# The residual's x read from HBM into the residual's own tile, nine of sixteen tiles during the gate stage

## What is computed

```python
h = rmsnorm(x, g_mix)
proj = h @ w_in                                   # 2048 -> u (1024) | v (1024) | z (1024)
u, v = gelu(u), gelu(v)
out_a = u * (tril(W_s) @ rmsnorm_per_head(v) + b) # chunks of 128 positions, 8 heads
out_b = (pool(z) @ w_pool) * pool_scale           # trailing means over 2/4/8/16, minus the token
x = x + concat(out_a, out_b) @ w_out              # the residual that the change touches
h = rmsnorm(x, g_ffn)
x = x + square(relu(h @ w_up)) @ w_down           # 2048 -> 8192 -> 2048
return rmsnorm(x, g_final)
```

## Time and profile before

| | us |
|---|---|
| time, median of 3 runs | 1242.95 (1240.61 to 1244.18) |
| the profiled execution's own time | 1238.04 |
| its span, slowest core (0) | 1236.2 |
| spans of the eight cores | 1229.5 to 1236.2 |
| TensorE busy | 1193.5 (97% of the span) |
| VectorE / ScalarE / GpSimd busy | 354.9 / 221.0 / 78.8 |
| output projection of core 0, about | 212 to 330 |

### The profile page before, as it was taken

One profiled execution on the slowest core, in us unless ns is written; L12 is line 12 of the kernel. 1 busy time (PEld: TensorE's weight loads), 2 busy tenths in 40 slices (PEclk: granted clock), 3 DMA queues, 4 the chain that ended last, 5 costly groups with the idle time before them and its releaser, 6 DMA issues.

```text
span 1236.2 us, 14873 instructions; the slowest of 8 cores (1229.5 to 1236.2 us)
## 1 busy us (share of the span) xinstructions
PE 1193.5 (97%) x5880; PEld 571.5 (46%) x5984; DVE 354.9 (29%) x587; ACT 221.0 (18%) x446; POOL 78.8 (6%) x107
## 2 busy tenths in 40 slices
PE   4899999989999999999999999999999999999996
PEld 2354444434444444444444444444444444444585
DVE  3466646333322121111112121212121212121254
ACT  2401155133321100001111000111100011111233
POOL 0100022100000000000000000000000000010000
PEclk9999999999999999999999999999999999999998
DMA  9995640987533443344334443444334433446033
GB/s 271 232 183 76 83 83 2 145 168 173 127 69 68 83 88 68 68 77 93 70 69 73 91 76 68 70 86 83 69 68 85 85 69 69 81 81 111 26 125 124
DMA packets 36755, 118.59 MB, mean 96 GB/s; under 512 B 2768, under 2 KB 5200, under 8 KB 35664
## 3 DMA queue, kind: packets, MB, share of 16 engines
q0 software_dynamic: 22736, 87.04, 41.0%
q1 hardware_dynamic: 13376, 29.43, 7.5%
q10 hardware_dynamic: 576, 1.18, 0.3%
HBM read 196.28 MB, written 8.39 MB: 166 GB/s over the span
## 4 chain that ended last, share of the span: by engine, by line
PE 92%; DMA 5%; DVE 1%; issue 1%; SPq 1%; ACT 0%; DVEq 0%; ACTq 0%
PE ps L226 83%; PE ps L672 6%; DMA xstage<-xT 3%; DMA xf<-xT 2%; PE ps L412 1%; PE ps L896 1%; SPq L244 0%; PE ps L324 0%; PE ps L546 0%; DVE ostage L925 0%; PE ps L363 0%; SPq L248 0%; DVE xr_h L679 0%; PE ps L709 0%; DVE xr_h L883 0%
## 5 line engine op out<-in xcount | busy, mean ns | idle before, releaser
L226 PE MATMUL ps<-h2T,ringall 128*128 128x512 bf16 x2008 | 440.7, 379 | 2.1
L226 PEld LDWEIGHTS ps<-h2T,ringall 128*128 128x128 bf16 x2048 | 200.4, 98 | 241.6
L226 PE MATMUL ps<-pooled,ringall 128*128 128x512 bf16 (+1 forms) x989 | 212.1, 362 | 1.0
L226 PE MATMUL ps<-uT,ringall 128*128 128x512 bf16 (+1 forms) x992 | 212.1, 362 | 0.8
L804 DVE SCALAR_TENSOR_TENSOR rtmp<-ps,rstd_bc 128x512 f32<-128x512 f32 x128 | 82.4, 686 | 361.3 <-PE ps L226 350.0
L226 PEld LDWEIGHTS ps<-pooled,ringall 128*128 128x128 bf16 x1008 | 98.6, 98 | 101.9
L226 PEld LDWEIGHTS ps<-uT,ringall 128*128 128x128 bf16 x1008 | 98.5, 98 | 101.9
L809 ACT ACTIVATE uT<-rtmp 128x512 bf16<-128x512 f32 x64 | 39.1, 629 | 504.6 <-DVE rtmp L804 504.5
L226 PE MATMUL ps<-hT,ringall 128*128 128x512 bf16 x375 | 82.6, 379 | 0.6 <-issue 0.2
L809 ACT ACTIVATE pooled<-rtmp 128x512 bf16<-128x512 f32 x64 | 39.2, 629 | 181.8 <-DVE rtmp L804 181.8
L226 PEld LDWEIGHTS ps<-hT,ringall 128*128 128x128 bf16 x384 | 37.2, 98 | 44.4
(11 more groups left out here) (117 smaller groups left out, 624.6 us busy)
## 6 DMA issues: line engine op xcount, KB each, us to landing
ringall<-w_up POOLq DMA_DIRECT2D x32, 1024.0 KB, 8.0
ringall<-w_down POOLq DMA_DIRECT2D x29, 1024.0 KB, 7.9
ringall<-w_in POOLq DMA_DIRECT2D x10, 1024.0 KB, 12.6
xf<-xT SPq DMA_DIRECT2D x8, 1024.0 KB, 20.6
xstage<-xT SPq DMA_DIRECT2D x16, 512.0 KB, 10.0
ringall<-w_out POOLq DMA_DIRECT2D x7, 1024.0 KB, 17.2
wstg<-w_in SPq DMA_DIRECT2D x4, 1024.0 KB, 16.4
wres<-w_down POOLq DMA_DIRECT2D x3, 1024.0 KB, 22.1
```

The costliest lines, as they stand in the source:

```text
L226: ins = e.matmul(ps[:, banks[sel], c0:c1], lhsT, rhs, start=st, stop=sp_)
```

## The change

Two things. The destination: x of tile m is read into `XR(m)` itself for m = 3 to 15, and the evacuation adds the PSUM bank to it in place. Tiles 0, 1 and 2 keep a staging buffer, the two old ones and a third, `xs2`, which lies over `sqr` (the buffer of squares, not in use between the first norm's sums and the second's). The time of issue: nine loads (tiles 0, 1, 2, 4, 5, 6, 7, 8, 9) are issued one behind the other at `pool_all`, early in the gate stage; tile 3's when the last v projection has read `hT` (`h_dead`); and tiles 10 to 15 together when tile 3 has been evacuated and its matmuls have read `wx`. Each load has a semaphore of its own. The number of loads and their bytes stay as they are.

```diff
+    xs2 = sb("xs2", [128, TOK], F32, cur[0] - 4096)
...
-    xs_reader = [pool_all, pool_all]
+    def XS(m):
+        return (xstage[0][:, :], xstage[1][:, :], xs2[:, :])[m] if m < 3 else XR(m)
+
     xs_ld = {}
 
-    def load_xs(m):
-        xs_ld[m] = P.dma("sp", lambda e: e.dma_start(out=xstage[m % 2][:, :].rearrange("p (h t) -> p h t", h=2), in_=xT_d[:, :, m, :]),
-                         "xs%d" % (m % 2), [xs_reader[m % 2]])
-
-    for m in range(2):
-        load_xs(m)
+    def load_xs(m, deps):
+        xs_ld[m] = P.dma("sp", lambda e: e.dma_start(out=XS(m).rearrange("p (h t) -> p h t", h=2), in_=xT_d[:, :, m, :]), "xs%d" % m, deps)
+
+    for m in (0, 1, 2, 4, 5, 6, 7, 8, 9):
+        load_xs(m, [pool_all, sq_reader[2], sq_reader[3]])
+    load_xs(3, [h_dead])
...
-        ev = P.add("dve", lambda e: e.tensor_tensor(out=XR(m)[:, c0:c1], in0=ps[:, bank, :], in1=xstage[m % 2][:, c0:c1], op=ALU.add),
+        ev = P.add("dve", lambda e: e.tensor_tensor(out=XR(m)[:, c0:c1], in0=ps[:, bank, :], in1=XS(m)[:, c0:c1], op=ALU.add),
                    [job, xs_ld[m], h_dead, pool_all])
...
         if half == 1:
-            xs_reader[m % 2] = x1_e[1][m]
-            if m + 2 < KC:
-                load_xs(m + 2)
+            if m == HEAD:
+                for i in (10, 11, 12, 13, 14, 15):
+                    load_xs(i, [x1_e[1][m], h_dead, job])
             wo_norm(m)
```

## The result

| | before | after |
|---|---|---|
| time, median of 6 runs, us | 1242.55 | 1232.6 |
| range of the comparable runs, us | 1239.9 to 1244.2 | 1232.2 to 1234.3 |
| ratio (95% interval) | | 0.9926 (0.991 to 0.9942) |
| the profiled execution's own time, us | 1238.04 | 1232.2 |
| spans of its eight cores, us | 1229.5 to 1236.2 | 1227.8 to 1230.3 |

The medians are over all six runs, with one slow run on either side (1324.8 and 1371.9 us) that the range and the ratio leave out. By the ratio the change makes the kernel 0.74% faster (0.58 to 0.9%), about 9.2 us.

The account below looks back on a forecast made before the run. The prediction took staging's loop of evacuation and late x loads to stop TensorE in the output projection. Stops and clock gave -5.5 us, the rest 0: 1242.95 to 1237.4 us, range 1234.0 to 1241.7.

Parts of the forecast that it names:

- What bounds the kernel: Output projection: evacuation, load through full queues and later evacuation form a loop that stops TensorE; core 0's excess 5.52 us.
- the floor: Matmuls behind the last mixing to first up matmul: 97.62 us on core 5, without waits for evacuation.
- the remainder: First up matmul to the span's end: about 906 us, the same to within 0.5 us whenever it starts.
- In place costs nothing: Evacuation adding into the residual's tile keeps its pace; 0 to 1 ns on each of 32 instructions.
- the nine loads are covered: Gate stage: 3.67 MB more, all in by about 191, covered by idle DMA from 170 to 212; cost nothing.
- the six come in time: Tiles 10 to 15, issued about 242.2: last lands about 270, at worst 309, each at least 14 us early.
- the slabs are not starved: Output projection: weight slabs 15, 16 and 17 land before tiles 8 and later need them, without stops too.
- The sum: -5.5 us for stops and clock, 0 for the rest; 4.9 us between profiled execution and median taken as unaffected.
- Rival (b): More than the whole: the 4.9 us are longer stops of the same kind; gain 7 to 10 us, chance 0.14.
- (a): Less than the whole: the typical slowest core is slow for another reason; gain 0 to 3.7 us, chance 0.17.
- (c): Slower: the six x loads starve the weights, TensorE stops at tile 8; +4 us, 1247, chance 0.05.
- (d): Some x, say tile 3's, is still late and the stop moves; about no change, 1242 us, chance 0.03.

Follow-up runs that it names:

- lower-group: Executions of the unchanged kernel before between 1234.7 and 1238.7 us: 33 of the study's 68 comparable ones.
- upper-group: Executions of the unchanged kernel before between 1239.4 and 1245.7 us: 35 of the study's 68 comparable ones.
- e10: The kernel before, unchanged, profiled a third more time to catch a slow execution; 1242.58 us.
- e7: The changed kernel with x of tile 14 issued late on purpose, when tile 14's matmuls are done; 1237.63 us.
- e3: The changed kernel with the loads of tiles 3 to 9 issued together at h_dead instead of in the gate stage; 1232.42 us, ratio 0.9945.
- e4: The kernel before with a third staging buffer, loads three tiles ahead, nothing in place; ratio 0.9945, six of seven runs 1232.4 to 1232.7 us.
- e2: The changed kernel's in-place reads, but each load issued at its time in the kernel before; median 1241.95 us, ratio 1.0007.
- e9: The kernel before, unchanged, profiled a second more time; 1236.12 us.

## Why the prediction was right in its mechanism and wrong in its size

The loop of staging, load and evacuation and its stops for banks were read rightly. A second stop that comes of the same lag, the one for the squares, was missed, and with it the size.

**What bounds the kernel, the floor, the remainder**: right. The stretch is 97.56 us after (97.62 forecast as floor), the rest 906.35, and the profiled execution's forecast of 1232.5 is the median after.

**In place costs nothing; the nine loads are covered; the six come in time; the slabs are not starved**: right. On core 2 tiles 10 to 15 landed by 245.7 + 25.9 = 271.6 (270 taken), 17 us and more before their needs, and slab 17 at 230.6 + 26.3 = 256.9, earlier than the 262.1 of the earlier trace rows. Tile 3's load, issued at 211.1, took 4.0 us. Only the issue of the nine was off: not done at 154 but at 166.6, as single issues took up to 7.4 us instead of 0.54. Nothing stood behind them but tile 3's load, which was not due before 211.

**The sum**: this step failed. "I take them as unaffected", of the 4.9 us between the profiled execution and the median, had no row behind it, and they were nearly all of the same cause: 5.5 us was the loss of the worst core in a lower-group execution, and the runs that the median came from were upper-group. Rival (b) came near, time 1233 to 1236 with 0.14, but with the wrong mechanism: it priced one more stop for a bank, 3.9 us. What the runs show is a stop for the squares, 5.0 us of idle time in e10, 2.5 to 3.9 us in e7, with about 1.5 us of clock behind it. Core 6 of e10 lost 1240.7 - (226.71 + 97.56 + 906.35) = 10.1 us: stops of 1.99, 0.38 and 4.96, 0.45 for modelled ends, 0.65 and 1.07 for the slower matmuls behind the last stop (1.68 and 8.14 us against 1.03 and 7.07), and 0.6 that I can't assign.

That the miss came out as large as it did is in part the luck of the sample. All five comparable runs of the kernel before in the result are of the upper group, while of all 68 about half are; against the mixed sets of e3 and e4 the same time of 1232.4 to 1232.5 us is a gain of 0.55%, some 7 us. So the forecast's gain of 5.5 us was that of a lower-group execution, the measured 9.2 us is that of upper-group ones, and a typical mixture lies between.

**The row that was there to be read.** I followed TensorE's stops and stopped at the last one, 272. On core 0 that was the end of it. Core 6 of the same trace, on which the prediction used only TensorE's rows, had VectorE still waiting for x at the end:

```profile
313.26 1.29 DVE L679 TENSOR_TENSOR xr_h<-ps,xstage 128x512 f32<-128x512 f32 x2 [7.54 <-DMA xstage<-xT]
...
322.01 1.29 DVE L679 TENSOR_TENSOR xr_h<-ps,xstage 128x512 f32<-128x512 f32 x2 [3.79 <-DMA xstage<-xT]
...
325.33 1.22 DVE L718 TENSOR_TENSOR sqr<-sqacc,sqr 128x1024 bf16<-128x1024 f32 x1
```

```profile
327.87 1.03 PE L709 MATMUL ps<-sqr,ones 128*128 128x512 bf16 x4
```

322.01 is tile 14. The squares were ready at 325.33 + 1.22 = 326.55, and TensorE took up their sum at 327.87. This core was 1.3 us from the edge. A wait that ended just in time on one core of this execution was, in e10, the stop that set the time.

**The other rivals.** (a), less than the whole, (c), starved slabs, and (d) did not come. Against (a) the prediction said that the order of the spans is the order of the loss; that holds for the three cores that it shows and not for all eight (core 3 lost 1.8 us in the stretch and core 1 only 1.0, yet core 1's span is the longer, as its stretch began later). For (c), e3, which put seven x loads right ahead of the slabs, is the harder test, and it didn't come there either.

What stays open: why an execution is in the lower or the upper group. The lag begins with x loads of 15 to 22 us beside the four slabs, and their times differ by a few us from core to core; what decides them was not tried. Upper-group executions were traced twice only (e10, and e2 core 4 of the kernel in place at the old times). Nor was it tried to add up tile 13's squares on VectorE ahead of tile 14's evacuation, which would test the stop for the squares with the staging buffers left alone.

## What to carry to other kernels

A double buffer whose refill waits for its reader can keep the lag that one crowded stretch gives it, when refill and evacuation beside other traffic take about as long as the work that they cover (14.0 and 12.9 us against 13.8 in e10). Here one more buffer (e4), or an issue that waits for no reader (e3), ended it, and e4 is by far the smaller change for the same time. Price a stall by the spread between executions, not by one trace: compare the trace's own time with the runs, and where it is lower, look on all cores for waits that ended just in time, down to the last consumer. And an order in program text can make a late operand reach a result that doesn't need it, as the squares did behind tile 14.

## What the runs showed of the hardware that was not expected

- A load of 512 KB took 4.0 us alone (tile 3, after), 5.0 to 8.5 one at a time beside the weights' steady stream (core 0 of e10), up to 12.5 in pairs beside it (core 6 of e10), and 22.3 beside four slabs.
- Nine such loads one behind the other on SP (core 2, after): single issues took up to 7.4 us instead of 0.54, the last began at 166.6 where the first was at 148.4.
- An idle time of 2.07 us was followed by matmuls at the lower clock; one of 2.12 us (core 1 of e9) and one of 2.58 us (core 6 of e2, granted clock 1.00 behind it) were not. In e7 the waits of 2.5 to 3.9 us on seven cores were (granted clock 0.83 in 326.9:337 on core 2), the one of 2.8 us on core 4 was not (1.00 in 324.4:334). The length of the stop alone does not tell whether the clock falls.
